# Two subtractions of 512 columns for one of 1024: splitting weights beside TensorE in the first expert passes of a two-layer decoder

## The chip, the cores and the metric

The kernel runs on one core of one Trainium2 chip. The metric is the device time of one launch in microseconds (us), the median of the runs. A profile is one execution, recorded by the hardware profiler; its span runs from the first to the last instruction that it shows. The engines are PE (TensorE: matmuls; PEld is its loading of weights), DVE (VectorE), ACT (ScalarE), POOL (GpSimd) and SP, which here only issues transfers.

## The reference

Two decoder layers over 256 tokens of width 2048, all in float32. Layer 0 uses stick-breaking attention, layer 1 latent attention; each layer ends with an expert network, and that is where the change lies:

```python
def peer_ffn(h, w_q, keys_1, keys_2, expert_u, expert_v):
    q = (h @ w_q).reshape(b, s, PEER_HEADS, 2, PEER_HALF)
    s1 = jnp.einsum('bshd,hkd->bshk', q[..., 0, :], keys_1)
    s2 = jnp.einsum('bshd,hkd->bshk', q[..., 1, :], keys_2)
    v1, i1 = lax.top_k(s1, PEER_TOPK)            # 16 of 128 keys, twice
    v2, i2 = lax.top_k(s2, PEER_TOPK)
    ...                                          # best 16 of the 256 sums: ids, softmax gates g
    u = jnp.take(expert_u, idx, axis=0)
    act = jax.nn.gelu(jnp.einsum('ced,cd->ce', u, hx), approximate=False)
    vv = jnp.take(expert_v, idx, axis=0)
    return jnp.einsum('ce,ced->cd', gx * act, vv)
```

There are 8 heads and 16,384 experts in each layer.

## The kernel before

**Products in two parts.** A float32 product is made of three products in a reduced format (fp32r): a weight tile `raw` is rounded to `hi`, the remainder is `lo = raw - hi`, activations are held as high and low parts too, and TensorE adds high by high, high by low and low by high.

**The stream of weights.** All weights are cut into 683 units of 128x2048 numbers, which SP loads in order into four slots of `raw` (`load`). A unit has two halves of 1024 columns. ScalarE rounds a half to `hi` (`split_hi`, line 665), VectorE or GpSimd makes `lo` (`split_lo`, line 1080, and line 574), TensorE uses both. There are four slots of `hi` and of `lo`, that is, two units. ScalarE may fill a slot when TensorE is done with the half before in it (`used`); VectorE may make `lo` when `hi` is there (`hi_ready`); a slot of `raw` comes free when both `lo` halves are made (`lo_ready`).

**The expert network** of a layer is two passes over 128 tiles of 128 experts, one unit for a tile. In the first pass TensorE multiplies the `expert_u` unit with all tokens (`unit_a`, lines 1718 for high and 1721 for low); tiles alternate between two banks. VectorE adds the two parts of a finished bank and so frees it (`sum_tile`, line 1384, semaphore `a_free`), then scales (1386); ScalarE applies gelu (839). In the second pass TensorE multiplies with `expert_v` (lines 1930, 1932, 1934). Which halves GpSimd takes is set by `gpsimd_takes`: in the first passes none, since it issues the indirect transfers that scatter the gates (606, 621, 630) and gather rows (595). So VectorE makes every `lo` there.

**VectorE's order in the first pass** is written out by hand. For tile j: the two `lo` halves of unit j + 2; `sum_tile(j)`; if one is due, a routing step (`route_step`); if one is due, a dot product over gathered rows (`dot`, line 1394). The routing steps are the top-16 search in the keys of one half of a head (`route_unit`, lines 1245 to 1260), the search among the 256 sums (`route_pairs`, the same lines), and the decoding of the positions found (`decode`, with 1303, 1307 and 1311 as its three operations of 1024 columns). They fall due every third tile, to tile 76; the dots every 3.4 tiles, to tile 105.

**TensorE's waits there.** Before tile j + 2 it waits for `a_free` of tile j (`unit_a`), and for `hi_ready` and `lo_ready` of the halves that it uses.

Of the kernel before, what the change touches and what calls it, by code (L numbers as in the profile page):

```python
# [29 lines left out]
F32 = mybir.dt.float32  # L30
# [5 lines left out]
ALU = mybir.AluOpType  # L36
# [18 lines left out]
HALF = UNIT // 2  # L55
RAW_SLOTS = 4
HALF_SLOTS = 4
LEAD = 2
TILES = NKEYS
# [60 lines left out]
def starts(table):  # L120
    out, n = {}, 0
    for name, count in table:
        out[name] = n
        n += count
    return out, n


U0, N_UNITS = starts(PHASE_UNITS)
# [13 lines left out]
def weight_gains(n0):  # L142

    if U0["c"] <= n0 < U0["c"] + 4:
        return G_KV + 4 * (n0 - U0["c"]), 512
    if U0["dq"] <= n0 < U0["dq"] + 4:
        return G_MLA + 4 * (n0 - U0["dq"]), 512
    return None


def gain_pieces(n0, j):

    gains = weight_gains(n0)
    if gains is None:
        return None
    col, width = gains
    n = HALF // width
    return [(col + n * j + q, slice(q * width, (q + 1) * width)) for q in range(n)]
# [14 lines left out]
def final_piece(i):  # L173

    width = D * NC_TOK // FINAL_PIECES
    c, q = divmod(i, FINAL_PIECES // NC_TOK)
    return c, slice(width * q, width * (q + 1))
# [69 lines left out]
def build_program(nc, x, x_t, positions, stream, keys, gains, final_g, inv_freq, u_rows0, u_rows1, peer_g, out):  # L247
    with ExitStack() as ctx:
        def sem(name):
            return ctx.enter_context(nc.semaphore(name))  # L250

        def sb(name, shape, dt=F32):
            return ctx.enter_context(nc.sbuf_tensor(name, shape, dt))
# [20 lines left out]
        hi = sb("hi", [P, HALF_SLOTS, HALF], F32R)  # L274
        lo = sb("lo", [P, HALF_SLOTS, HALF], F32R)
# [126 lines left out]
        lo_ready = [sem(f"lo_ready{i}") for i in range(HALF_SLOTS)]  # L402
# [66 lines left out]
        def halves(n0):  # L469

            for j in range(2):
                h = 2 * n0 + j
                yield j, h % HALF_SLOTS, h // HALF_SLOTS

        def gpsimd_takes(n0, s):

            if weight_gains(n0) is not None:
                return False
            if any(U0[f"wq{k}"] + POOL_UNTIL <= n0 < U0[f"peer{k}"] + TILES for k in range(2)):
                return False  # L480
            if U0["kn"] + 2 <= n0 < U0["mwo"]:
                return s % 2 == 1
            busy = any(U0[f"wq{k}"] + LEAD <= n0 < U0[f"wq{k}"] + POOL_UNTIL for k in range(2))
            return s % 2 == 1 if busy else s == HALF_SLOTS - 1

        def unit_done(engine, n0):

            *_, (_, s, k) = halves(n0)
            engine.wait_ge(used[s], k + 1)
# [57 lines left out]
        def _(pool):  # L547
# [21 lines left out]
            def split_lo(n0):  # L569

                for j, s, k in halves(n0):
                    if gpsimd_takes(n0, s) and n0 < N_UNITS:
                        pool.wait_ge(hi_ready[s], k + 1)
                        pool.tensor_tensor(lo[:, s, :], raw[:, n0 % RAW_SLOTS, j * HALF:(j + 1) * HALF],  # L574
                                           hi[:, s, :].bitcast(F32), ALU.subtract).then_inc(lo_ready[s], 1)
# [494 lines left out]
        def _(dve):  # L1070
            steps = Steps(dve, dve_step)

            def split_lo(n0, parts=(0, 1)):
                for j, s, k in halves(n0):
                    if not gpsimd_takes(n0, s) and n0 < N_UNITS and j in parts:
                        dve.wait_ge(hi_ready[s], k + 1)
                        half = raw[:, n0 % RAW_SLOTS, j * HALF:(j + 1) * HALF]
                        pieces = gain_pieces(n0, j)
                        if pieces is None:
                            dve.tensor_tensor(lo[:, s, :], half, hi[:, s, :].bitcast(F32),  # L1080
                                              ALU.subtract).then_inc(lo_ready[s], 1)
                        else:
                            for col, at in pieces:
                                ins = dve.scalar_tensor_tensor(
                                    out=lo[:, s, at], in0=half[:, at], scalar=gain_t[:, col:col + 1],
                                    in1=hi[:, s, at].bitcast(F32), op0=ALU.mult, op1=ALU.subtract)
                            ins.then_inc(lo_ready[s], 1)
# [105 lines left out]
            def output_product(phase, rows_phase, col, begun=0):  # L1193

                first = U0[phase]
                for q in range(QUARTERS):
                    for j in range(begun if q == 0 else 0, 3):
                        split_lo(first + 4 * q + j + LEAD)
                        if j == 0 and q >= 1:
                            rows_lo(rows_phase, 2 * q - 2, col)  # L1200
                            rows_lo(rows_phase, 2 * q - 1, col)
                    last = first + 4 * q + 3
                    add_block(B0[phase] + q, 512 * q, last)
                    split_lo(last + LEAD)
                rows_lo(rows_phase, KT // 2 - 2, col)
                rows_lo(rows_phase, KT // 2 - 1, col)
# [155 lines left out]
            def peer(layer):  # L1362
# [50 lines left out]
                for j in range(TILES):  # L1413
                    split_lo(base + j + LEAD)
                    sum_tile(j)
                    route_step(layer, 2 * PEER_HEADS + j)
                    if j in DOTS:
                        dot(DOTS[j])
                    if j in PAIR_COEFS:
                        weigh_pairs(PAIR_COEFS[j])  # L1420
                    if j >= TILES - GROUP:
                        prepare(j - TILES)
# [112 lines left out]
            for i in range(STEPS):  # L1535
# [20 lines left out]
                if i < HEADS:  # L1556
# [3 lines left out]
                    for lo_col, hi_col in ((0, P), (P, LIVE)):  # L1560
                        back = slice(hi_col - 1, lo_col - 1 if lo_col else None, -1)
                        ins = dve.tensor_tensor_scan(sp_[:, back], sp_[:, back], tmp[:, back], 0.0, ALU.add, ALU.add)
# [69 lines left out]
            for w in range(2):  # L1632
                r = slice(ROPE * w, ROPE * (w + 1))
                ins = dve.tensor_copy(kr_t[r, w, :], ps_c[C0["krt"] % 2][r, 0:S])
# [24 lines left out]
            for s in range(ML_SLOTS):  # L1659
# [15 lines left out]
                if h is not None:  # L1675
# [3 lines left out]
                    for c, (lo_col, hi_col) in enumerate(((0, P), (P, LIVE))):  # L1679
                        pr = ml_p[:, h % 3, lo_col:hi_col]  # L1680
                        ins = dve.tensor_scalar(pr, pr, m_[:, 6 + c:7 + c], None, ALU.mult)
# [10 lines left out]
            for i in range(FINAL_PIECES):  # L1692
                c, at = final_piece(i)
# [549 lines left out]
```

## Time and profile before

| what | value |
|---|---|
| time, median of 3 runs | 3638.71 us (3636.71 to 3639.38) |
| the profiled execution | 3635.06 us, its span 3633.2 us |
| mean granted clock of TensorE | 0.996 of full |
| busy: PE, DVE, ACT, POOL | 98%, 62%, 50%, 41% |
| first pass of layer 0, of layer 1 | about 494 to 1177 us, 2238 to 2923 us |
| VectorE's `lo` halves (line 1080) | 1077, mean 1235 ns |

The profile's views are read like this. The page gives busy time by engine and the chain of work that ended last, followed back from the end. The views by stretch (windows) give the busy time of each engine in a stretch, with the granted clock. The view of waits says who waited for whom. The timeline lists instructions by start and duration, runs of one instruction merged as xN; an instruction can start before the one in front of it on the same engine has ended, so durations of neighbours overlap.

### The profile page before, as it was taken

How to read it: one execution, taken by the hardware profiler on the slowest of the kernel's cores; microseconds unless marked ns; L12 is line 12 of the kernel's file. 1: busy time of each engine (PE TensorE's matmuls, PEld its weight loads, DVE VectorE, ACT ScalarE, POOL GpSimd, SP SyncE). 2: the span in 40 equal slices, each digit the busy share in tenths (PEclk: the TensorE clock that was granted, in tenths of full speed). 3: DMA queues.
4: the chain of work that ended last, by engine and by line, in shares of the span. 5: the costliest groups of instructions: out<-in, count | busy, mean ns of one | idle time of the engine just before them, and what ended most of it. 6: DMA issues, size and time to landing. Idle time of an engine off the chain costs nothing.

```text
span 3633.2 us, 48916 instructions
## 1 busy us (share of the span) xinstructions
PE 3559.6 (98%) x19088; PEld 3124.5 (86%) x19088; DVE 2266.3 (62%) x3437; ACT 1807.4 (50%) x2646; POOL 1502.6 (41%) x796
## 2 busy tenths in 40 slices
PE   8999999999999999999999999999999999999998
PEld 7888888888999888888889888898899988888887
DVE  5565588898876444444456557888887654444444
ACT  4365455555555444444455545555555544444443
POOL 2211366777784222222212126687778612222221
PEclk9999999999999999999999999999999999999999
DMA  9844578888887888877754357888888766666674
GB/s 350 286 158 165 201 248 264 269 266 273 285 268 242 284 281 279 281 263 238 240 188 163 116 205 231 266 271 265 263 284 280 241 244 237 240 240 229 242 243 167
DMA packets 327479, 886.46 MB, mean 244 GB/s; under 512 B 123728, under 2 KB 226128, under 8 KB 235344
## 3 DMA queue, kind: packets, MB, share of 16 engines
q1 hardware_dynamic: 132992, 718.38, 55.2%
q0 software_dynamic: 83232, 69.51, 10.1%
q10 hardware_dynamic: 111024, 95.44, 8.0%
q8 instruction: 151, 2.47, 0.3%
q14 instruction: 80, 0.66, 0.0%
HBM read 817.95 MB, written 65.27 MB: 243 GB/s over the span
## 4 chain that ended last, share of the span: by engine, by line
PE 88%; DVE 9%; issue 1%; ACT 1%; ACTq 0%; DMA 0%; DVEq 0%; SPq 0%
PE banks L1718 24%; PE banks L1721 13%; PE banks L1930 13%; PE banks L1934 13%; PE banks L1932 13%; PE banks L1748 3%; PE banks L1750 3%; PE banks L1749 3%; DVE lo L1080 3%; DVE pair_rows L1394 1%; ACT hi L665 1%; DVE stage L1384 1%; DVE match L1307 0%; DVE hit L1303 0%; DVE sel_f L1311 0%
## 5 line engine op out<-in xcount | busy, mean ns | idle before, releaser
L665 ACT ACTIVATE hi<-raw 128x1024 fp32r<-128x1024 f32 x1278 | 1352.2, 1060 | 1608.4 <-PE banks L1934 697.0
L1080 DVE TENSOR_TENSOR lo<-raw,hi 128x1024 fp32r<-128x1024 f32 x1077 | 1317.3, 1235 | 1176.1 <-ACT hi L665 1166.2
L574 POOL TENSOR_TENSOR lo<-raw,hi 128x1024 fp32r<-128x1024 f32 x201 | 483.9, 2407 | 1755.7 <-ACT hi L665 1755.7
L1718 PE MATMUL banks<-act_t,hi 128*128 128x448 f32 (+1 forms) x5120 | 1140.6, 374 | 59.8 <-DVE stage L1384 48.9
L1718 PEld LDWEIGHTS banks<-act_t,hi 128*128 128x128 f32 x5120 | 939.2, 189 | 168.1 <-DVE stage L1384 62.5
L1721 PEld LDWEIGHTS banks<-act_t,lo 128*128 128x128 f32 x5120 | 636.0, 193 | 15.7 <-issue 2.3
L1721 PE MATMUL banks<-act_t,lo 128*128 128x224 f32 (+1 forms) x5120 | 643.5, 277 | 1.1 <-DVE lo L1080 1.1
L1930 PE MATMUL banks<-hi,wa 128*128 128x512 f32 x2024 | 623.2, 389 | 0.0
L1932 PE MATMUL banks<-lo,wa 128*128 128x512 f32 x2024 | 623.1, 389 | 0.0
L1934 PE MATMUL banks<-hi,wa 128*128 128x512 f32 x2024 | 623.1, 389 | 0.0
L621 POOL DMA_INDIRECT w_rows<-gate,place_u x256 | 467.0, 1824 | 167.1 <-issue 80.7
L1930 PEld LDWEIGHTS banks<-hi,wa 128*128 128x128 f32 x2024 | 379.8, 188 | 79.2 <-issue 0.6
L1932 PEld LDWEIGHTS banks<-lo,wa 128*128 128x128 f32 x2024 | 379.9, 188 | 78.9
L1934 PEld LDWEIGHTS banks<-hi,wa 128*128 128x128 f32 x2024 | 379.9, 188 | 78.9
L630 POOL DMA_INDIRECT w_rows<-late_gate,late_u x192 | 345.6, 1800 | 58.5 <-issue 58.2
L1394 DVE CUSTOM_DVE_ANT_0 pair_rows<-pair_rows,banks 128x2048 f32<-128x2048 f32 x64 | 145.9, 2280 | 0.0
L606 POOL DMA_INDIRECT pair_w<-pair_coef,pair_u x64 | 119.6, 1869 | 19.5 <-issue 19.5
L595 POOL DMA_INDIRECT pair_rows<-in_u_rows,pair_u x64 | 82.3, 1286 | 105.3 <-DVE pair_dot L1394 64.1
L839 ACT ACTIVATE stage<-stage 128x224 f32<-128x224 f32 x256 | 96.0, 375 | 31.9 <-DVE stage L1386 21.2
L1386 DVE TENSOR_TENSOR stage<-stage,inv_row 128x224 f32<-128x224 f32 x256 | 103.1, 403 | 8.9
L1384 DVE TENSOR_TENSOR stage<-banks,part 128x224 f32<-128x224 f32 x256 | 98.1, 383 | 13.5 <-ACT part L833 13.5
L1748 PE MATMUL banks<-hi,ot_t 128*128 128x512 f32 x256 | 101.2, 395 | 1.3 <-DVE mv_tok L1175 1.3
(262 smaller groups left out, 2437.8 us busy)
## 6 DMA issues: line engine op xcount, KB each, us to landing
raw<-in_stream SPq DMA_DIRECT2D x647, 1024.0 KB
w_rows<-zeros SPq DMA_DIRECT2D x64, 448.0 KB, 9.6
act_rows<-stage ACTq DMA_DIRECT2D x64, 448.0 KB
acts<-act_rows ACTq DMA_DIRECT2D x64, 448.0 KB, 4.2
w_part<-w_rows ACTq DMA_DIRECT2D x64, 448.0 KB, 7.8
pair_w<-zeros SPq DMA_DIRECT2D x4, 1024.0 KB, 11.4
w_rows<-gate,place_u POOLq DMA_INDIRECT x256
acts<-pair_w ACTq DMA_DIRECT2D x64, 64.0 KB, 4.3
```

Of the source, the lines that this page charges most:

```text
L574: pool.tensor_tensor(lo[:, s, :], raw[:, n0 % RAW_SLOTS, j * HALF:(j + 1) * HALF], hi[:, s, :].bitcast(F32), ALU.subtract).then_inc(lo_rea ...
L621: pool.indirect_dma_start(rows, bass.IndirectOffsetOnAxis(ap=place_u[:, 0, k:k + 1], axis=0), gate[:, 0, k:k + 1], None, compute_op=ALU.ad ...
L630: pool.indirect_dma_start(rows, bass.IndirectOffsetOnAxis(ap=late_u[:, k:k + 1], axis=0), late_gate[:, k:k + 1], None, compute_op=ALU.add) ...
L665: act.activation(hi[:, s, :], half, ACT.Copy).then_inc(hi_ready[s], 1)
L1080: dve.tensor_tensor(lo[:, s, :], half, hi[:, s, :].bitcast(F32), ALU.subtract).then_inc(lo_ready[s], 1)
L1394: dve.tensor_tensor_reduce(pair_rows[b][:], pair_rows[b][:], normed_pairs, 1.0, 0.0, ALU.mult, ALU.add, pair_dot[:, j:j + 1]).then_inc(dot ...
L1718: ins = mm(both, hi[:, s, at], act_t[:, kt, :, 0:tokens], start=(kt == 0), stop=(kt == KT - 1), skip_group_check=True)
L1721: ins = mm(ps[:, 0:tokens], lo[:, s, at], act_t[:, kt, 0, 0:tokens], start=False, stop=False, skip_group_check=True)
L1748: mm(o, a_hi, w_hi, start=(kt == 0), stop=False)
L1930: mm(o[:], a_hi, hi[:, s, at], start=first, stop=False)
L1932: mm(o[:], a_hi, lo[:, s, at], start=False, stop=False)
L1934: ins = mm(o[:], a_lo, hi[:, s, at], start=False, stop=last)
```

## The change

In the units from peer0 + 2 to peer0 + 127 and from peer1 + 2 to peer1 + 127 (the first passes), VectorE makes each `lo` half with two instructions of 512 columns. Only the second one raises `lo_ready`. The two units at the head of each pass are left as they are. The new function `first_pass` says which units these are.

```diff
+        def first_pass(n0):
+            return any(U0[f"peer{k}"] + LEAD <= n0 < U0[f"peer{k}"] + TILES for k in range(2))
...
                         if pieces is None:
-                            dve.tensor_tensor(lo[:, s, :], half, hi[:, s, :].bitcast(F32),
-                                              ALU.subtract).then_inc(lo_ready[s], 1)
+                            width = HALF // 2 if first_pass(n0) else HALF
+                            for at in (slice(a, a + width) for a in range(0, HALF, width)):
+                                ins = dve.tensor_tensor(lo[:, s, at], half[:, at], hi[:, s, at].bitcast(F32),
+                                                        ALU.subtract)
+                            ins.then_inc(lo_ready[s], 1)
```

On VectorE, around the first decoding step of layer 0's first pass, the program before has this order (`lo` halves at 1080, the sum that frees a bank at 1384):

```order
L1080 TENSOR_TENSOR lo<-raw,hi 128x1024 x2
L1384 TENSOR_TENSOR stage<-banks,part 128x224
L1386 TENSOR_TENSOR stage<-stage,inv_row 128x224
L1297 TENSOR_SCALAR pos_u<-sel_p 128x32
L1298 TENSOR_SCALAR pos_u<-sel_p 128x32
L1299 CAST top_f<-top_i 128x64
L1301 CAST pos_f<-pos_u 128x64
L1303 TENSOR_TENSOR hit<-pos_f,ranks 128x1024
```

The changed program has, at the same place (its lines behind the change are numbered 6 or 7 higher):

```order
L1086 TENSOR_TENSOR lo<-raw,hi 128x512 x4
L1391 TENSOR_TENSOR stage<-banks,part 128x224
L1393 TENSOR_TENSOR stage<-stage,inv_row 128x224
L1304 TENSOR_SCALAR pos_u<-sel_p 128x32
L1305 TENSOR_SCALAR pos_u<-sel_p 128x32
L1306 CAST top_f<-top_i 128x64
L1308 CAST pos_f<-pos_u 128x64
L1310 TENSOR_TENSOR hit<-pos_f,ranks 128x1024
```

Two instructions became four, and nothing changed places. In the whole program 504 halves become 1008 instructions; the other 573 halves of VectorE stay whole. The other engines' instructions are the same, in the same order.

## Rows read from the trace of the kernel before

**Rows 1.** The page: busy time of each engine, and the chain by engine
```profile
PE 3559.6 (98%) x19088; PEld 3124.5 (86%) x19088; DVE 2266.3 (62%) x3437; ACT 1807.4 (50%) x2646; POOL 1502.6 (41%) x796
...
PE 88%; DVE 9%; issue 1%; ACT 1%; ACTq 0%; DMA 0%; DVEq 0%; SPq 0%
```

**Rows 2.** Busy time by stretch: the first passes, with and without routing steps
```profile
core 0: us, PE busy (x) PEld busy (x) DVE busy (x) ACT busy (x) POOL busy (x), PEclk, DMA share, GB/s
508.00:932.00 424.00, 402.05 (x2516) 376.25 (x2515) 382.74 (x776) 244.12 (x467) 304.10 (x180) 0.99 0.86 269
932.00:1177.00 245.00, 242.72 (x1539) 230.03 (x1538) 170.93 (x216) 127.97 (x196) 167.79 (x88) 1.00 0.85 264
2252.00:2680.00 428.00, 406.02 (x2528) 379.77 (x2527) 385.01 (x781) 245.65 (x470) 307.25 (x180) 0.99 0.86 269
```

**Rows 3.** TensorE's waits, 508 to 932 us: total us, times, longest
```profile
PE banks L1718 <- DVE stage L1384: 21.9, 13, 3.1
```

**Rows 4.** The chain of waits, pieces from 508 to 532 us: start, us, what
```profile
508.97 0.02 issue
...
514.99 1.49 DVE lo L1080 x2
...
520.29 0.81 DVE lo L1080
...
521.34 1.22 DVE lo L1080
...
528.47 2.27 DVE lo L1080 x2
...
531.09 1.09 PE banks L1718 x4
```

**Rows 5.** The chain by line, 508 to 932 us
```profile
by line: PE banks L1718 35.1%; PE banks L1721 18.9%; DVE lo L1080 11.3%; issue 5.7%; DVE pair_rows L1394 4.8%; ACT hi L665 3.0%; DVE stage L1384 2.5%; DVE hit L1303 2.0%; DVE match L1307 2.0%; DVE sel_f L1311 2.0%; PE banks L1841 1.3%; ACT 
```

**Rows 6.** VectorE's timeline: start, us, instructions, at four places
```profile
50.74 2.11 DVE L1514 TENSOR_TENSOR qk_t<-qk_t,inv_row 128x256 f32<-128x256 f32 x6
...
528.38 2.36 DVE L1080 TENSOR_TENSOR lo<-raw,hi 128x1024 fp32r<-128x1024 f32 x2
...
1872.67 1.28 DVE L1146 TENSOR_TENSOR act_t<-banks,act_t 128x512 fp32r<-128x512 f32 x2
...
1875.15 1.41 DVE L1084 SCALAR_TENSOR_TENSOR lo<-raw,gain_t,hi 128x512 fp32r<-128x512 f32 x2 [1.20 <-ACT hi L668]
```

**Rows 7.** Durations of single instructions: ns min/median/max, first and last start
```profile
L1080 DVE TENSOR_TENSOR lo<-raw,hi x1077: 1204/1225/3407, 9.6 to 3612.7; 128x1024 fp32r<-128x1024 f32 x180
...
L1084 DVE SCALAR_TENSOR_TENSOR lo<-raw,gain_t,hi x32: 743/746/753, 1869.5 to 1918.2; 128x512 fp32r<-128x512 f32 x32
...
L1146 DVE TENSOR_TENSOR act_t<-banks,act_t x8: 680/684/692, 1870.8 to 1886.3; 128x512 fp32r<-128x512 f32 x8
...
L1514 DVE TENSOR_TENSOR qk_t<-qk_t,inv_row x6: 418/418/428, 50.7 to 52.4; 128x256 f32<-128x256 f32 x6
```

**Rows 8.** TensorE's timeline behind two stalls
```profile
563.95 1.89 PE L1718 MATMUL banks<-act_t,hi 128*128 128x448 f32 x8 [1.41 <-DVE stage L1384]
...
567.46 3.43 PE L1718 MATMUL banks<-act_t,hi 128*128 128x448 f32 x16
...
581.58 2.44 PE L1718 MATMUL banks<-act_t,hi 128*128 128x448 f32 x8 [2.21 <-DVE stage L1384]
...
586.69 3.42 PE L1718 MATMUL banks<-act_t,hi 128*128 128x448 f32 x16
```

**Rows 9.** One stretch with a lower granted clock
```profile
576.00:600.00 24.00, 20.98 (x123) 19.28 (x122) 20.14 (x37) 13.47 (x21) 20.34 (x13) 0.93 0.79 240
```

**Rows 10.** GpSimd's indirect transfers, and ScalarE's first load for the second pass
```profile
601.47 1.54 POOL L621 DMA_INDIRECT w_rows<-gate,place_u  x1 [0.30 <-issue]
...
1135.96 2.17 POOL L630 DMA_INDIRECT w_rows<-late_gate,late_u  x1 [0.30 <-issue]
...
1149.90 0.59 ACTq L781 DMA_DIRECT2D acts<-act_rows  x1
```

## The prediction

> **What bounds the kernel now.** I read the busy times and the chain first. TensorE is busy for 98% of the span, VectorE for 62%, and yet the chain of work that ended last runs over VectorE for 9% [rows 1]. So there are places where VectorE sets the time though it idles on the average, and the next view must say where. Busy time by stretch shows it: while routing steps run in the first passes (508 to 932 us and 2252 to 2680 us) VectorE is busy for 382.74 of 424 and 385.01 of 428 us, 90%, and TensorE loses 424 - 402.05 = 22.0 us and 428 - 406.02 = 22.0 us; behind that, in 932 to 1177 us, VectorE is at 70% and TensorE loses 2.3 us [rows 2]. The waits name the cause: 21.9 us in 13 waits, all for the sum at line 1384, which frees a bank [rows 3]. The reader should see that this is the whole loss. TensorE never waits there for `lo` itself; `lo` matters since its halves stand in VectorE's queue ahead of that sum.
>
> The chain shows how such a wait comes about. From 508.97 to 531.09 us it leaves TensorE, and runs through ScalarE, six `lo` halves, sums, a dot and the decoding step, back to TensorE [rows 4]. I counted these detours: 24 in both passes (the first is that one, and the last begins at 2647.09 us), and 103 `lo` halves in them. By shares the same: 11.3% of 424 us is 47.9 us in layer 0 [rows 5], layer 1's stretch is alike, and 96 us at 1.135 us a half is 84 whole halves; the rest are halves of which only a part shows, as the 0.81 us piece [rows 4].
>
> **What the change does.** It removes 504 subtractions of 1024 columns and adds 1008 of 512. Columns, data and order stay; the semaphore comes with the second piece, so nothing is released earlier. What can change is the fixed cost of an instruction, paid once more per half.
>
> That cost is read from starts, not from durations, since neighbours overlap. One half: two of them take 2.36 us to the end of the second [rows 6], and the chain gives them 2.27 us, which is when the next instruction starts [rows 4]; so 1.135 us from start to start, though one lasts 1.225 us [rows 7]. For 512 columns there are three readings:
> - Line 1146, two pieces of 512 with one input in a bank: 1.28 - 0.684 = 0.596 us from start to start [rows 6, 7]. Two make 1.19, so +0.06 us per half.
> - Line 1514, six instructions of 256 columns with both inputs where `lo` has them: (2.11 - 0.418) / 5 = 0.338 us [rows 6, 7]. On the line between 256 and 1024 columns, 512 take 0.338 + (1.135 - 0.338) / 3 = 0.604 us, so +0.07 us.
> - Line 1084, which makes a scaled `lo` in two pieces of 512: 1.41 - 0.746 = 0.66 us, so +0.19 us [rows 6, 7]. It has a third operand, and I take it as an upper end only.
>
> The first two are the nearest in kind. I take +0.065 us per half. The lower end is 0 (the second piece needs no wait of its own and might follow without any gap); another end is that the pieces don't overlap at all: 2 x 0.684 - 1.225 = +0.143 us [rows 7].
>
> The sum:
> - VectorE's work grows by 504 x 0.065 = 33 us. Most of it lies beside TensorE's work, in gaps in which VectorE waits for `hi`.
> - On the path are the 103 halves of the detours: 103 x 0.065 = 6.7 us.
> - Short pauses of VectorE in front of these detours close, and a few sums that are now just in time come late. Counting the halves since VectorE's last pause of any size, at each wait of TensorE, gives some 115 instead of 103: + 12 x 0.065 = 0.8 us.
> - The clock. After the stall of 2.21 us, TensorE takes 586.69 - 581.58 = 5.11 us for 8 + 16 matmuls that take 567.46 - 563.95 = 3.51 us after the stall of 1.41 us [rows 8]; the stretch around it has a granted clock of 0.93, which over 24 us is 3.4 us at the lower level of 1.2 GHz [rows 9]. So a dip costs 1.6 us. Five of the ten stalls above 2 us that VectorE causes are followed by one. Stalls become 0.2 to 0.5 us longer, so I add 0.4 of a dip, 0.6 us.
> - GpSimd. Its indirect transfers take 1.54 us at one place and 2.17 us where VectorE is at its `lo` halves all along, and its last one of layer 0's first pass starts at 1135.96 us, while ScalarE turns to the loads that need it at 1149.90 us [rows 10]. Some 12 us of slack cover any change there, to either side: 0.
> - SP's loads wait for `lo_ready`, 0.06 us later on a slot used once in four units: 0.
>
> Together 6.7 + 0.8 + 0.6 = 8.1 us. The profiled execution, 3635.06 us, would become 3643.2 us. It lies 3.65 us under the median of the runs shown, and the same 8.1 us on 3638.71 us give 3646.8 us.
>
> A page of the Trainium skill speaks against so small a price. "VectorE: DVE Perf Modes", section "The TRN2 errata", gives the duration of a float32 tensor_tensor as (N + 151) / 0.96 ns, and says that the latency is exposed between instructions, so that many small tiles pay it each time. The durations of this trace agree: (1024 + 151) / 0.96 = 1224 ns against 1225, (512 + 151) / 0.96 = 691 against 684 (one input in a bank there) [rows 7]. Taken as the time that each piece occupies the engine, it would be an estimate of +157 ns per half and, over 115 halves, +18 us. "Perfetto Trace Analysis", section "Optimizing Scalar/DVE Operations", says otherwise: about 60 ns of engine time per instruction, the profiled latency being about twice this since the end overlaps with the next one; the estimate by it is 115 x 0.06 = 7 us. The starts in rows 6 side with the second page; the first page's way is rival B.
>
> **The rivals.**
>
> B, the pieces don't overlap. For: every duration has the fixed part of some 150 ns. Against: line 1146's pair, and the half itself, start 0.09 us before their forerunner's end. Price: 115 x 0.143 = 16.4 us, and one more dip, 1.6: 3638.7 + 18 = 3656.7 us.
>
> C, not slower: the dips go. All stalls move against one another, and whether one is followed by a dip isn't decided by its length alone: the one of 2.21 us is, while others of 3 us aren't. Five dips are 8.0 us. Where four or five of them vanish and VectorE pays no more than 0.065 us a half, the loss is made up: 3638.7 + 7.5 - 8.0 = 3638 us. It decides from four dips on. The milder form is that the second piece costs 0.03 us or less, since it waits for nothing: 115 x 0.03 = 3.5 us, 3642 us. Against this form is again line 1146's pair, where there is no wait between the pieces either. I put C at 3640 us.
>
> D, the dips multiply. 24 detours, all longer: if three more stalls are followed by one, and these bring sums late in turn, 7.5 + 3 x 1.6 = 12.3, so 3651 us. For: ten stalls above 2 us become some twelve. Against: during a dip VectorE catches up with TensorE.
>
> E, faster: GpSimd gets at its memory between the pieces and its transfers of 2.17 us become 1.54 us. For: the difference between the two figures. Against: nobody on the chain waits for GpSimd there, so there is nothing to win; for a gain the gathered rows or the scatters would have to be late now. 3636 us at the most.
>
> That the change doesn't do what it says I exclude: the order shows 252 rows of four pieces in the first passes, where GpSimd takes no half.
>
> **How the numbers follow.** Forecast 0.52; B 0.11; C 0.20; D 0.12; E 0.05. The forecast's own range is 3643 to 3651 us (0.05 to 0.08 us a half, a dip fewer or more). The range that should hold the time 8 times in 10 reaches from C's middle to B: 3640 to 3657 us. About 0.2% (7.3 us) is what a measurement of this kernel can tell from no change, and that is under the forecast's 8.1 us by little, so of its 0.52 some 0.33 lie above 3646.0 us and 0.19 below. Slower: 0.33 + B 0.11 + D 0.12 = 0.56. Within: 0.19 + C 0.20 = 0.39. Faster: 0.05.
>
> **What the profile after would show.** The pieces have a median duration of 0.68 to 0.69 us; four of them, from the first one's start to that of the sum behind, take about 2.40 us (B: 2.56; C's milder form: 2.30). VectorE is busy 504 x (2 x 0.69 - 1.225) = 78 us longer by the durations, which is more than it loses, since they overlap. TensorE's waits for the sum grow from 21.9 to about 26 us in each pass, in the same places; the second passes and the attention keep their times. The number of stretches at the lower clock separates D and C from the forecast. The forecast is wrong if the pieces start 0.60 us apart and TensorE's waits don't grow, or if the loss lies outside the two stretches with routing steps.

## The result: 9.5 us slower, where it was forecast

| | runs | median us | range | ratio to before, 95% interval |
|---|---|---|---|---|
| before | 14 | 3637.63 | 3634.59 to 3642.16 | |
| changed | 14 | 3647.15 | 3642.99 to 3651.33 | 1.0024 [1.0016, 1.0032] |

The forecast was 3646.8 us. The profiled execution of the changed kernel took 3650.09 us with a span of 3648.3 us, so it lies 3 us above its median, while the one of before lay under its own; the spans of the two traces are 15.1 us apart. What that surplus is, is part of the answer.

The page of the changed kernel, the rows that answer to [rows 1] and the groups of VectorE's `lo` and GpSimd's transfers (columns: busy us and mean ns, then idle before):

```profile
PE 3568.8 (98%) x19088; PEld 3132.5 (86%) x19088; DVE 2301.1 (63%) x3941; ACT 1807.4 (50%) x2646; POOL 1407.9 (39%) x796
...
PE 87%; DVE 10%; ACT 1%; issue 1%; ACTq 0%; DMA 0%; DVEq 0%; SPq 0%
...
L1086 DVE TENSOR_TENSOR lo<-raw,hi 128x512 fp32r<-128x512 f32 (+1 forms) x1581 | 1352.2, 889 | 1157.9 <-ACT hi L669 1156.7
...
L625 POOL DMA_INDIRECT w_rows<-gate,place_u x256 | 428.7, 1674 | 173.8 <-issue 80.8
```

VectorE has 504 instructions more and a point more of the chain. Its busy time grew by 2301.1 - 2266.3 = 34.8 us. GpSimd's busy time fell by 94.7 us.

TensorE's waits over the whole kernel; first the kernel before, then the changed one (total us, times, longest):

```profile
PE banks L1718 <- DVE stage L1384: 48.9, 27, 3.1
```

```profile
PE banks L1725 <- DVE stage L1391: 54.5, 33, 3.2
```

The wait is the same, for the sum that frees a bank, and 5.6 us longer in sum. No wait of another kind appeared. The view counts the waits of the loading of weights apart; for this sum they are 6.2 us longer, first before, then changed:

```profile
PEld banks L1718 <- DVE stage L1384: 62.5, 38, 3.4
```

```profile
PEld banks L1725 <- DVE stage L1391: 68.7, 38, 3.6
```

By stretch, as in [rows 2] (the changed kernel runs some us later, so the second stretch ends later; columns as there):

```profile
508.00:932.00 424.00, 400.07 (x2472) 373.96 (x2471) 385.14 (x914) 238.49 (x447) 278.22 (x177) 0.98 0.82 265
932.00:1185.00 253.00, 249.55 (x1584) 236.25 (x1583) 185.35 (x329) 134.21 (x217) 145.88 (x91) 1.00 0.83 263
```

In 508 to 932 us TensorE got through 2472 matmuls in place of 2516, and the granted clock is a point lower. VectorE's timeline at the detour of [rows 4], with four pieces in place of two:

```profile
529.60 2.49 DVE L1086 TENSOR_TENSOR lo<-raw,hi 128x512 fp32r<-128x512 f32 x4
532.00 0.38 DVE L1391 TENSOR_TENSOR stage<-banks,part 128x224 f32<-128x224 f32 x1
```

From the first piece to the sum 532.00 - 529.60 = 2.40 us, against 2.27 us before: 0.065 us per half. The chain there, from TensorE and back to it (start, us, what):

```profile
509.91 0.02 issue
...
529.68 2.41 DVE lo L1086 x4
532.09 0.31 DVE stage L1391
532.40 0.04 issue
532.44 1.69 PE banks L1725 x7
```

It took 532.44 - 509.91 = 22.53 us, before 531.09 - 508.97 = 22.12 us: 0.41 us for six halves, 0.07 us each.

**The clock.** A stall is sometimes followed by a stretch of 3.4 us at the lower level, in the first passes of the changed trace eleven times, in the trace of before six times (one each of them behind the wait at the end of layer 1's first pass, which has another cause). TensorE's timeline behind two stalls of the changed kernel:

```profile
852.42 1.90 PE L1725 MATMUL banks<-act_t,hi 128*128 128x448 f32 x8 [2.36 <-DVE stage L1391]
854.16 1.94 PE L1728 MATMUL banks<-act_t,lo 128*128 128x224 f32 x16
...
871.05 3.23 PE L1725 MATMUL banks<-act_t,hi 128*128 128x448 f32 x8 [3.23 <-DVE stage L1391]
874.08 1.31 PE L1728 MATMUL banks<-act_t,lo 128*128 128x224 f32 x8
```

Eight matmuls take 1.90 us behind the one and 3.23 us behind the other. Before, the stall at that second place had no such stretch behind it:

```profile
864.27 1.90 PE L1718 MATMUL banks<-act_t,hi 128*128 128x448 f32 x8 [3.05 <-DVE stage L1384]
```

The last wait of each pass left aside, both traces have ten stalls above 2 us. Before, five of them are followed by such a stretch; in the changed kernel seven are, and so are three of four stalls of 1.86 to 1.98 us, a length that doesn't occur before. Five stretches more, at the prediction's 1.6 us each, are 8.0 us. With the 6.2 us of waits they make 14.2 of the 15.1 us between the two traces. That waits and clock may be added like this is a reading of the traces; no run separates them.

Every execution comes with its mean granted clock, and so the two effects can be parted over many runs too. Sorted by it, the means are:

| mean clock | before, us (runs) | changed, us (runs) | difference |
|---|---|---|---|
| 0.994 | 3641.4 (2) | 3649.4 (4) | 7.9 |
| 0.995 | 3639.0 (9) | 3647.2 (6) | 8.2 |
| 0.996 | 3636.2 (13) | 3644.1 (4) | 8.0 |

(Before: 24 of the 26 runs taken beside E1 to E6; the other two had 0.997. The 14 runs of before in the first table have no clock on record.) At the same clock the change costs 8.1 us; within a kernel 0.001 of the clock goes with 2.7 us, and the changed kernel's mean clock is 0.0006 lower, 1.6 us. Together 9.7 us, against 9.5 us between the medians. The clock is on record to 0.001 only, which is 2.7 us, so this division is no finer than some 2 us; why it gives 8.1 us at the same clock where the waits grew by 5.6 to 6.2 us stays open. The profiled execution of the changed kernel had a clock of 0.994, that of before 0.996, which is why they lie further apart.

### The profile page after: what moved, and what is told of

Same layout as the page of the kernel before. It is cut to its first block, busy times and chain, and to the rows that moved or that the text cites. A ratio compares the mean times of both kernels' runs of the same rounds, so it can differ in the third digit from the quotient of the medians.

```text
span 3648.3 us, 49420 instructions
## 1 busy us (share of the span) xinstructions
PE 3568.8 (98%) x19088; PEld 3132.5 (86%) x19088; DVE 2301.1 (63%) x3941; ACT 1807.4 (50%) x2646; POOL 1407.9 (39%) x796
## 4 chain that ended last, share of the span: by engine, by line
PE 87%; DVE 10%; ACT 1%; issue 1%; ACTq 0%; DMA 0%; DVEq 0%; SPq 0%
PE banks L1725 23%; PE banks L1937 13%; PE banks L1939 13%; PE banks L1941 13%; PE banks L1728 12%; DVE lo L1086 4%; PE banks L1755 3%; PE banks L1757 3%; PE banks L1756 3%; DVE pair_rows L1401 1%; ACT hi L669 1%; DVE stage L1391 1%; DVE hit L1310 0%; DVE match L1314 0%; DVE sel_f L1318 0%
## 5 line engine op out<-in xcount | busy, mean ns | idle before, releaser
L1086 DVE TENSOR_TENSOR lo<-raw,hi 128x512 fp32r<-128x512 f32 (+1 forms) x1581 | 1352.2, 889 | 1157.9 <-ACT hi L669 1156.7
L1725 PE MATMUL banks<-act_t,hi 128*128 128x448 f32 (+1 forms) x5120 | 1145.7, 375 | 65.7 <-DVE stage L1391 54.5
L625 POOL DMA_INDIRECT w_rows<-gate,place_u x256 | 428.7, 1674 | 173.8 <-issue 80.8
L634 POOL DMA_INDIRECT w_rows<-late_gate,late_u x192 | 314.9, 1640 | 58.5 <-issue 58.5
L599 POOL DMA_INDIRECT pair_rows<-in_u_rows,pair_u x64 | 73.6, 1150 | 153.8 <-DVE pair_dot L1401 102.4
L610 POOL DMA_INDIRECT pair_w<-pair_coef,pair_u x64 | 102.5, 1601 | 19.5 <-issue 19.5
```

Of the source, the lines that this page charges most:

```text
L625: pool.indirect_dma_start(rows, bass.IndirectOffsetOnAxis(ap=place_u[:, 0, k:k + 1], axis=0), gate[:, 0, k:k + 1], None, compute_op=ALU.ad ...
L634: pool.indirect_dma_start(rows, bass.IndirectOffsetOnAxis(ap=late_u[:, k:k + 1], axis=0), late_gate[:, k:k + 1], None, compute_op=ALU.add) ...
L1086: ins = dve.tensor_tensor(lo[:, s, at], half[:, at], hi[:, s, at].bitcast(F32), ALU.subtract)
L1725: ins = mm(both, hi[:, s, at], act_t[:, kt, :, 0:tokens], start=(kt == 0), stop=(kt == KT - 1), skip_group_check=True)
```

## The experiments

**E1: four pieces of 256.**

```diff
-                            width = HALF // 2 if first_pass(n0) else HALF
+                            width = HALF // 4 if first_pass(n0) else HALF
```

> Each lo half of the first passes in four instructions of 256 columns (2016 in all). Theory T (a fixed engine time of 0.07 us per added instruction, paid on the path by the halves that stand ahead of a late sum, plus some more dips of the clock): three added instructions per half instead of one, 3 x 0.07 x 115 = 24 us and 3 to 8 us of dips over before, ratio 1.0075 (1.006 to 1.010); eight 256-column pieces start to sum 2.27 + 6 x 0.07 = 2.69 us; waits of TensorE for the sum about 33 to 35 us per pass. Rival R (the loss comes once with the splitting as such, e.g. by the semaphore's piece or by how GpSimd and VectorE share memory, not per instruction): ratio as of the changed kernel, 1.0024 to 1.004.

Measured: 3675.56 us, ratio 1.0103 [1.0087, 1.0118]. The price is per instruction, and R is refuted. VectorE's timeline, eight pieces and the sum behind:

```profile
530.84 2.76 DVE L1086 TENSOR_TENSOR lo<-raw,hi 128x256 fp32r<-128x256 f32 x8
533.52 0.38 DVE L1391 TENSOR_TENSOR stage<-banks,part 128x224 f32<-128x224 f32 x1
```

They take 2.68 us to the sum, 2.69 us was expected, so 0.068 us per added instruction. But the time rose by more than theory T's 24 us and dips: 38 us. The waits:

```profile
PE banks L1725 <- DVE stage L1391: 73.3, 44, 3.7
```

They are 24.4 us longer than before, which is T's sum, and there are 44 in place of 27: sums that came in time are now late. Its four executions have a mean clock of 0.9928, 0.0028 under before, which by the slope above is some 7.5 us. That leaves about 6 us. The trace itself accounts for more. At the loading of weights the waits for the sum are 27.7 us longer than before:

```profile
PEld banks L1725 <- DVE stage L1391: 90.2, 46, 4.1
```

And the lower clock was granted thirteen times in its first passes, seven times more than before, 11.2 us at 1.6 us each. Together that is 38.9 us, and the spans of the two traces are 39.1 us apart.

**E2 and E3: only where there are routing steps, and only where there are none.**

```diff
-            return any(U0[f"peer{k}"] + LEAD <= n0 < U0[f"peer{k}"] + TILES for k in range(2))
+            return any(U0[f"peer{k}"] + LEAD <= n0 < U0[f"peer{k}"] + 80 for k in range(2))      # E2
+            return any(U0[f"peer{k}"] + 80 <= n0 < U0[f"peer{k}"] + TILES for k in range(2))     # E3
```

> Only the halves of units 2 to 79 of both first passes are split in two (312 halves of 504). Theory T: all of the loss is here, ratio 1.0024 as of the changed kernel. Rival S (every split half costs something, wherever it is): 312/504 of it, 1.0015. TensorE's waits for the sum: T 27 us per pass as in the changed kernel.

> Only the halves of units 80 to 127 of both first passes are split in two (192 halves of 504). Theory T: VectorE has gaps there, ratio 1.0000 (0.9995 to 1.0005), waits of TensorE for the sum as before, 24 us per pass. Rival S (every split half costs something): 1.0009.

Measured: E2 3647.86 us, ratio 1.0029 [1.0018, 1.0039]; E3 3636.66 us, ratio 0.9998 [0.9989, 1.0007]. The loss comes with 312 of the 504 halves; the other 192 show none, with an upper end of 2.5 us by the interval. Rival S's 1.0015 and 1.0009 lie outside the intervals, though by little. The waits decide it, first E2, then E3:

```profile
PE banks L1725 <- DVE stage L1391: 51.8, 29, 3.3
PE banks L1725 <- ACT hi L669: 9.9, 1, 9.9
PE banks L1725 <- issue: 2.5, 3, 1.5
```

```profile
PE banks L1725 <- DVE stage L1391: 48.0, 27, 3.1
```

E3 waits as the kernel before does (48.9 us, 27 times). E2 has 51.8 us and 2.5 us more without a releaser in the records, 54.3 us together, against 54.5 us in the changed kernel.

**E4: the same number of instructions, of 64 and 960 columns.**

```diff
-                            width = HALF // 2 if first_pass(n0) else HALF
-                            for at in (slice(a, a + width) for a in range(0, HALF, width)):
+                            cuts = (0, 64, HALF) if first_pass(n0) else (0, HALF)
+                            for at in (slice(*ends) for ends in zip(cuts, cuts[1:])):
```

> The same 504 halves in two instructions, but of 64 and 960 columns. Theory T: the fixed time is paid per instruction whatever its columns, ratio 1.0024 (1.0015 to 1.0035), 0.07 us per half in the detours. Rival G (GpSimd's shorter transfers, mean 1.82 us before and 1.67 us in the changed kernel, take part in the result): GpSimd's transfers go back to nearly 1.8 us here and the ratio differs from the changed kernel's, below 1.001 or above 1.004.

Measured: 3648.17 us, ratio 1.0031 [1.0018, 1.0043]. So how the columns are divided makes no difference that can be told; two halves take the same 2.41 us to the sum:

```profile
531.77 2.49 DVE L1086 TENSOR_TENSOR lo<-raw,hi 128x64 fp32r<-128x64 f32 x4
534.18 0.38 DVE L1391 TENSOR_TENSOR stage<-banks,part 128x224 f32<-128x224 f32 x1
```

(Four instructions of both shapes, merged under the first one's shape.) GpSimd's transfers did go back, beyond where they were. Before, E4, and then E1 and E8 (which comes below), both with pieces of 256 (columns as on the page):

```profile
L621 POOL DMA_INDIRECT w_rows<-gate,place_u x256 | 467.0, 1824 | 167.1 <-issue 80.7
```

```profile
L625 POOL DMA_INDIRECT w_rows<-gate,place_u x256 | 479.5, 1873 | 164.8 <-issue 79.3 <-DMA w_rows<-late_gate,late_u 63.8 <-DVE gate L1341 21.7
```

```profile
L625 POOL DMA_INDIRECT w_rows<-gate,place_u x256 | 428.1, 1672 | 182.3 <-issue 84.0
```

```profile
L625 POOL DMA_INDIRECT w_rows<-gate,place_u x256 | 459.4, 1795 | 166.2 <-issue 84.1
```

1873 ns with a piece of 960 columns, 1824 ns before, 1674 ns with pieces of 512, 1672 and 1795 ns with pieces of 256. So they don't simply follow the length of VectorE's instructions. The time doesn't follow them either: E4 has longer transfers than the kernel before and loses as the changed kernel does. Rival G is refuted.

**E5: the sum before the halves, where it is late.** Whole halves as in the kernel before:

```diff
                 for j in range(TILES):
-                    split_lo(base + j + LEAD)
-                    sum_tile(j)
+                    if 2 * PEER_HEADS + j - 1 in ROUTE_STEPS:
+                        sum_tile(j)
+                        split_lo(base + j + LEAD)
+                    else:
+                        split_lo(base + j + LEAD)
+                        sum_tile(j)
```

> The kernel before, whole halves, but in the tile behind each routing step of the first passes VectorE frees the bank (sum_tile) before it makes the two lo halves. Theory T (TensorE's waits there are two lo halves long because these stand ahead of the late sum): the sum comes 2.27 us earlier where it is late, lo of the first half is then 2.0 us behind the freeing of the bank, needed 1.66 + 0.42 us behind it; most of the 24 waits (22 us per pass) shrink by up to 2 us, the clock's dips go with them: 30 to 45 us faster, ratio 0.989 (0.987 to 0.993). Rival V (VectorE has simply too much work in these stretches, 90% busy, and order can't help): the waits turn up at lo (line 1080) instead, ratio 0.998 to 1.000.

Measured: 3592.8 us, ratio 0.9877 [0.9861, 0.9894], 44.5 us faster than before. So TensorE had waited for the sum that stood behind the `lo` halves, not for `lo`; rival V's waits for `lo` did not turn up. TensorE's waits, and VectorE behind the decoding step:

```profile
PE banks L1722 <- DVE stage L1384: 12.8, 10, 2.4
```

```profile
529.20 0.23 DVE L1326 SCALAR_TENSOR_TENSOR place_u<-sel_f,place_by,place_f 128x16 uint32<-128x16 f32 x1
529.35 0.38 DVE L1384 TENSOR_TENSOR stage<-banks,part 128x224 f32<-128x224 f32 x1
529.76 0.39 DVE L1386 TENSOR_TENSOR stage<-stage,inv_row 128x224 f32<-128x224 f32 x1
530.08 2.35 DVE L1080 TENSOR_TENSOR lo<-raw,hi 128x1024 fp32r<-128x1024 f32 x2
```

The waits fell by 36.1 us. The trace has one stretch at the lower clock left in both first passes, against six; five of 1.6 us are another 8 us. Together 44.1 us; the spans of the two traces are 45.4 us apart.

**E6: the sum first, with the halves in two pieces.**

> The same order, with every lo half of the first passes in two pieces as in the changed kernel. Theory T: with the sum ahead of the halves, the extra 0.07 us per half stands behind the freeing of the bank and mostly in VectorE's gaps: against the whole halves in the same order less than half of the loss, 0 to 4 us. Rival V (VectorE bound by its amount of work): the same 9 us or more between the two.

Measured: 3597.43 us, ratio 0.9891 [0.9874, 0.9907], so 4.6 us over E5, with intervals that overlap. That is just outside the 0 to 4 us of theory T and half of rival V's 9 us, and settles neither. Its waits are 15.2 us in 13 times against 12.8 in 10.

**E8: the sum first, with four pieces,** to have a larger step.

> The order with the sum first behind a routing step, and every lo half of the first passes in four pieces of 256. The order alone took 3592.8 us, with two pieces 3597.4 us, but the intervals of these two overlap. If halves on the path still pay there (VectorE bound by its amount of work in the stretches with routing steps), three added instructions cost about three times that difference or more: 3592.8 + 15 to 25 us, ratio 0.992 to 0.995. If the new order had taken the halves off the path, the time stays within 5 us of 3597: ratio 0.988 to 0.990.

Measured: 3635.92 us, ratio 0.9993 [0.9984, 1.0002]: 43 us over E5, far above both expectations, and of the gain of the new order nothing is left. TensorE's waits for the sum are back, E5's 12.8 us became

```profile
PE banks L1729 <- DVE stage L1391: 40.8, 56, 4.8
```

The likeliest reason is in VectorE's share of 508 to 932 us, E5 first and then E8:

```profile
508.00:932.00 424.00, 419.78 (x2655) 394.33 (x2654) 399.64 (x801) 254.10 (x486) 317.81 (x189) 1.00 0.90 284
```

```profile
508.00:932.00 424.00, 406.98 (x2521) 374.06 (x2520) 411.69 (x1239) 241.61 (x464) 306.69 (x180) 1.00 0.84 267
```

In the same 424 us TensorE gets through 134 matmuls less, 5%, which at E5's pace is 21 us in this stretch alone. In E5 VectorE is already busy for 399.64 of 424 us. Its waits for `hi`, its spare time, first E5 in this stretch and in layer 1's (2252 to 2680 us), then E8 in this one:

```profile
DVE lo L1080 <- ACT hi L665: 14.4, 20, 1.7
```

```profile
DVE lo L1080 <- ACT hi L665: 21.5, 27, 1.7
```

```profile
DVE lo L1086 <- ACT hi L669: 2.9, 4, 1.2
```

With four pieces it has next to none. 312 halves x 3 x 0.068 = 64 us of added work on 14.4 + 21.5 = 36 us of spare time leave 28 us; the other 15 us of the 43 would be spare time that doesn't lie where the work is, and I can't show that. This account was made after the result, and no run tests it by itself. As far as it holds, the new order takes the halves off the path only while VectorE has time left; behind it lies the bound by its amount of work, and there rival V is right.

**E7: the sum first behind the dot products too.**

```diff
-                    if 2 * PEER_HEADS + j - 1 in ROUTE_STEPS:
+                    if 2 * PEER_HEADS + j - 1 in ROUTE_STEPS or j - 1 in DOTS:
```

> Whole halves, and the sum first also in the tile behind each dot product (32 per pass), late or not. If VectorE is late there too, the last waits of TensorE for the sum (6.4 us per pass) shrink: up to 4 us faster than the order with routing steps alone, ratio 0.9866. If it is in time there, the sum has to wait for ScalarE's part of it with the lo halves queued behind, VectorE loses gaps that it needs, and it is slower: ratio 0.989 to 0.993.

Measured: 3589.93 us, ratio 0.9875 [0.9859, 0.9890]. From E5's 0.9877 this can't be told apart, and the interval holds the faster outcome and touches the slower one. The waits did not shrink: 14.2 us in 14 times against 12.8 us in 10. In 508 to 932 us VectorE's spare time is smaller (10.9 us against 14.4 us), and the sum waits longer for ScalarE's part (4.7 us against 2.4 us).

## Why the prediction was right

- **The place.** "This is the whole loss": TensorE waits for the sum, `lo` stands ahead of it. E5 shows it from the other side: with the halves behind the sum, three quarters of the waits go (48.9 us to 12.8 us). E2 and E3 show no loss outside the stretches with routing steps.
- **The price of a half.** Forecast 0.065 us, measured 0.065 to 0.07 us (2.40 and 2.41 us for two halves, 0.41 us in the detour of six). The two readings from starts, 0.06 and 0.07 us, enclosed it. The upper reading, from the scaled `lo` with its third operand, doesn't apply. Rival B (durations, 0.143 us) is refuted by the same rows: the pieces last 0.691 us in the median and start 0.60 us apart. The Trainium skill's (N + 151) / 0.96 ns ("VectorE: DVE Perf Modes", section "The TRN2 errata") holds for the duration (691 ns) and not for the engine's time; its section "Optimizing Scalar/DVE Operations" in "Perfetto Trace Analysis", about 60 ns with the rest overlapping, is the one that this case bears out.
- **The number on the path.** Forecast 115 halves, 12 of them by short pauses that close. The detours of the changed kernel's chain hold 228 pieces, 114 halves; in the chain before a recount gives 100, not 103. The 14 more all stand in the last detour of each pass, which begins earlier and holds 15 halves in place of eight. 114 x 0.07 = 8.0 us, and 8.1 us is what the runs show at the same clock; the waits alone show 5.6 to 6.2 us. E1's waits, 24.4 us longer, give 24.4 / (3 x 0.068) = 120.
- **The clock** was the term that was sized too small. I had put 0.4 of a dip, 0.6 us; in the trace there are five more, 8 us, and over all the runs 1.6 us. The step that the forecast missed is that shorter stalls, of 1.9 to 2.0 us, are followed by a dip too; stalls above 2 us were to become some twelve and stayed at ten. So rival D's mechanism is real and its size on the average 1.6 us, a third of D's 4.8 us (three dips of 1.6 us); in the profiled execution it was above D's. The number differs from trace to trace: 8 dips in the first passes in E4 and 11 in the changed kernel, with nearly the same waits (55.3 and 54.5 us). C, that the dips go, is not borne out: the five traces with split halves in the old order have 7 to 13, against six before. Its milder form (0.03 us a half or less) is refuted by the starts.
- **The closeness is luck.** The median, 3647.15 us, lies 0.35 us from the forecast of 3646.8 us. The loss was 9.5 us and not 8.1 us, and the kernel before came out 1.1 us lower than in the three runs that the 8.1 us were added to.
- **GpSimd.** The transfers did become shorter, 1674 ns from 1824 ns, as rival E had it; that GpSimd gets at its memory between the pieces is not shown. As argued, nobody waited for them, and E4 shows that the time doesn't depend on them. The prediction's reading of its two figures was loose: beside the transfer of 2.17 us VectorE made one half and a sum and had a pause of 0.6 us, it was not at its `lo` halves all along.
- **Two statements were wrong.** VectorE's busy time was to grow by 78 us by the durations. It grew by 34.8 us, since the view counts overlapping instructions once. 504 x 0.065 = 33 us, the work as first summed, was the right number for that view too. The waits grew by 2.8 us per pass and not by 4.

## What to carry to other kernels

Read the engine time of a small instruction from the starts of neighbours, not from its duration: here 0.60 us against 0.69 us, and the whole answer hangs on the 0.07 us that one more costs. An engine at 62% of the span can set the time where it is at 90%; then only instructions ahead of the late one count, so ask first whether they have to stand there, since moving a 0.4 us sum past two long instructions gave 44 us where splitting them lost 9.5. After such a step the same engine may be bound by its amount of work (E8 points to it), and then more of the small instructions are paid.

## What the runs showed of the hardware

- VectorE's float32 subtractions in SBUF: 1024 columns every 1.135 us, 512 every 0.60 us, 256 every 0.335 us, that is about 0.067 us beside the columns; durations 1.225, 0.691 and 0.418 us.
- GpSimd's indirect transfers change with VectorE's instructions beside them: in VectorE's old order 1672, 1674, 1824 and 1873 ns on the average beside pieces of 256, 512, 1024 and 960 (with 64) columns, but 1795 ns beside pieces of 256 in E8. That 960 with 64 is above 1024 alone, and why E8 differs from E1, I can't explain.
- A stall of TensorE of 1.9 to 3.2 us is sometimes followed by 3.4 us at the lower clock, and the same stall in another kernel isn't. Over executions of one kernel 0.001 of the mean clock goes with 2.7 us, and between 0.994 and 0.997 this accounts for most of the 9.2 us between the fastest and the slowest of the 26 runs of the kernel before.
